# Two weight splits moved from GpSimd to ScalarE and VectorE: gate's first unit, and v and k of the second attention

## What is computed

```python
h = rms_norm(x, pre_norm_gain);  q, k, v, z_a, b, c, u, z_c = split(h @ w_in)
attn = rms_norm(diff_attention(q, k, v)) * silu(z_a);  conv_out = b * conv(c * u) * silu(z_c)
mixed = concat(attn, conv_out) @ w_out
x = x + rms_norm(mixed, post_norm_gain)                 # x1
e = rms_norm(p @ w_ple_proj, ple_norm_gain)
x = x + sigmoid(x @ w_ple_gate) * e                     # x2
```

```python
y = gmlp(rms_norm(x, a_pre_g)) @ a_w_out                # a
h = x + rms_norm(y, a_post_g)                           # h3
kv = rms_norm(h, kv_norm_g);  k, v = kv @ w_k, kv @ w_v # k5, v5: 256 columns each
q, z = split(rms_norm(h, b_pre_g) @ b_w_in)             # q5, z5
out = h + rms_norm((swa(q, k, v) * silu(z)) @ b_w_out, b_post_g)
```

## Time and profile before

| | us |
|---|---|
| median of 3 runs | 880.46 |
| lowest, highest | 880.06, 880.82 |
| the profiled execution | 880.86 |
| its span, first to last instruction | 879.1 |
| TensorE busy | 863.0 (98%) |
| VectorE busy | 574.7 (65%) |
| GpSimd busy | 510.2 (58%) |
| ScalarE busy | 385.3 (44%) |

### The profile page before, as it was taken

One profiled execution on the slowest core, in us unless ns is written; L12 is line 12 of the kernel. 1 busy time (PEld: TensorE's weight loads), 2 busy tenths in 40 slices (PEclk: granted clock), 3 DMA queues, 4 the chain that ended last, 5 costly groups with the idle time before them and its releaser, 6 DMA issues.

```text
span 879.1 us, 11945 instructions
## 1 busy us (share of the span) xinstructions
PE 863.0 (98%) x4196; PEld 718.9 (82%) x4196; DVE 574.7 (65%) x918; ACT 385.3 (44%) x830; POOL 510.2 (58%) x564
## 2 busy tenths in 40 slices
PE   8999999999999999999999999999997999999997
PEld 6888888888887788888888888888887888888885
DVE  6125648875998389676766625556995467788624
ACT  4123333433665377555112311113775446667622
POOL 7766555682248822319974048772369797566352
PEclk9999999999999999999999999999999999999999
DMA  7543222453952468994742254526961222112202
GB/s 199 167 121 97 72 79 66 142 121 72 236 197 71 144 144 181 218 231 150 170 121 86 88 168 108 133 80 163 213 181 60 72 80 89 49 48 73 72 1 95
DMA packets 83691, 106.84 MB, mean 122 GB/s; under 512 B 11953, under 2 KB 54449, under 8 KB 83634
## 3 DMA queue, kind: packets, MB, share of 16 engines
q1 hardware_dynamic: 72752, 85.12, 30.5%
q0 software_dynamic: 10880, 20.97, 14.1%
q10 hardware_dynamic: 2, 0.00, 0.0%
HBM read 103.98 MB, written 2.10 MB: 121 GB/s over the span
## 4 chain that ended last, share of the span: by engine, by line
PE 88%; POOL 4%; DVE 4%; issue 1%; ACT 1%; DMA 1%; POOLq 0%; DVEq 0%; ACTq 0%
PE bank L2192 26%; PE bank L2194 26%; PE bank L2193 26%; PE bank L2436 2%; PE bank L2464 1%; DMA raw<-in_w_out 1%; DVE acc L1747 1%; PE bank L2289 1%; POOL wlo L873 1%; PE bank L2409 1%; PE bank L2459 1%; PE bank L2458 1%; DVE resid L1751 1%; POOL ms L818 1%; POOL whi L864 1%
## 5 line engine op out<-in xcount | busy, mean ns | idle before, releaser
L873 POOL TENSOR_TENSOR wlo<-raw,whi 128x512 fp32r<-128x512 f32 x184 | 254.8, 1417 | 3.9 <-ACT whi L1052 3.2
L864 POOL TENSOR_SCALAR whi<-raw 128x512 fp32r<-128x512 f32 x174 | 122.8, 746 | 175.7 <-PE bank L2194 170.1
L2192 PE MATMUL bank<-actB_hi,whi 128*128 128x512 f32 (+1 forms) x416 | 159.6, 384 | 0.6 <-POOL wlo L873 0.6
L2193 PE MATMUL bank<-actB_lo,whi 128*128 128x512 f32 (+1 forms) x416 | 158.6, 381 | 0.0
L2194 PE MATMUL bank<-actB_hi,wlo 128*128 128x512 f32 (+1 forms) x416 | 158.5, 381 | 0.0
L2192 PE MATMUL bank<-whi,actA_hi 128*128 128x512 f32 x350 | 138.0, 394 | 1.0 <-DVE actA_lo L1496 1.0
L2194 PE MATMUL bank<-whi,actA_lo 128*128 128x512 f32 x350 | 136.4, 390 | 0.0
L2193 PE MATMUL bank<-wlo,actA_hi 128*128 128x512 f32 x350 | 136.2, 389 | 0.0
L2192 PEld LDWEIGHTS bank<-actB_hi,whi 128*128 128x128 f32 x416 | 78.3, 188 | 15.5 <-issue 1.4
L2194 PEld LDWEIGHTS bank<-actB_hi,wlo 128*128 128x128 f32 x416 | 78.2, 188 | 15.2
L2193 PEld LDWEIGHTS bank<-actB_lo,whi 128*128 128x128 f32 x416 | 78.3, 188 | 14.2
(11 more groups left out here) (273 smaller groups left out, 1636.3 us busy)
## 6 DMA issues: line engine op xcount, KB each, us to landing
raw<-in_a_w_in SPq DMA_DIRECT2D x44, 512.0 KB, 4.3
raw<-in_w_in SPq DMA_DIRECT2D x32, 512.0 KB, 3.9
raw<-in_b_w_in SPq DMA_DIRECT2D x16, 512.0 KB, 3.4
raw<-in_a_w_out SPq DMA_DIRECT2D x12, 512.0 KB, 3.5
gain<-in_a_w_out POOLq DMA_DIRECT2D x9, 512.0 KB, 8.6
raw<-in_w_ple_gate SPq DMA_DIRECT2D x8, 512.0 KB, 4.6
gain<-in_a_w_in POOLq DMA_DIRECT2D x8, 512.0 KB, 7.0
raw<-in_a_w_in POOLq DMA_DIRECT2D x8, 512.0 KB, 7.4
```

What stands on the lines that cost most here:

```text
L864: pool.tensor_scalar(H, src[:, i * HALF:(i + 1) * HALF], 1.0, 1.0, ALU.mult, ALU.mult).then_inc(w_hi, 1)
L873: ins = pool.tensor_tensor(L, src[:, i * HALF:(i + 1) * HALF], H.bitcast(f32), ALU.subtract)
L2192: M(out_, whi_, xhi_, start=start, stop=False)
L2193: M(out_, whi_, xlo_, start=False, stop=False)
```

## The change

Two units change their path, and orders around them change with it.

- gate 0 goes to the path of ScalarE and VectorE (`hi_two`, and two `lo_two` ahead of `post`). GpSimd's roots of m1 (the sum that x1 needs) and its mask of w_s now all stand before gate 1.
- v5 and k5 go to that path as well. v5 is loaded into a room of its own, V (`smC` and `gcv`), right after a10's load. ScalarE scales v5 between the copies for a8, a9 and a10, copies it after a10, and scales k5 around the copy for a12. VectorE subtracts v5 after the residual of tile 1 and k5 after the low parts of n0 and a later gain. GpSimd runs its eight roots in a row.
- v5's loads wait for a11's to land and k5's for v5's, since they share the counts `room_in`, and GpSimd's scaling waits for a count of `w_scaled`.
- Orders: the block n0 of TensorE moves between the two blocks of a13, n1 stays behind it. On VectorE, sums, gains and residuals of each tile move closer together, and a13's second subtraction behind the first residual. On ScalarE, the copies of a13's two halves come behind the squares that the first roots need.

```diff
@@ weight tables
 BY_TWO = [n for n, u in enumerate(UNITS) if u[2] == "S"
-          or u[:2] in (("ple", 0), ("z4", 0), ("z4", 4))]
-TWO_NO = {n: k for k, n in enumerate(BY_TWO)}
+          or u[:2] in (("ple", 0), ("gate", 0), ("z4", 0), ("z4", 4))]
+V5_K5 = [n for s in ("v5", "k5") for n, u in enumerate(UNITS) if u[0] == s]
+HI_NO = {n: k for k, n in enumerate(BY_TWO[:-3] + V5_K5[:1] + BY_TWO[-3:] + V5_K5[1:])}
+TWO_NO = {n: k for k, n in enumerate(BY_TWO + V5_K5)}
@@ tensor_order
-        o += [("A", n, r) for n in (range(4), range(4, 14))[half] for r in range(2)]
-    o += turn("n", 0) + turn("n", 1) + [("v5", 0), ("v5", 1)]
+        o += [("A", n, r) for n in (range(4), range(4, 13))[half] for r in range(2)]
+    o += [("A", 13, 0)] + turn("n", 0) + [("A", 13, 1)] + turn("n", 1) + [("v5", 0), ("v5", 1)]
@@ room_place
+                    "V": gcv[:, :, :].rearrange("p a b -> p (a b)")[:, 0:D] if h else smC[:, :],
@@ SyncE, load_half
+                elif s == "v5":
+                    sp.wait_ge(s4_bias, KA)
+                    sp.wait_ge(zu_made, KA)
+                    sp.wait_ge(raw_in[10 + h], LANDED[UNIT_NO["a", 11], h])
...
+                if s == "k5":
+                    sp.wait_ge(raw_in[10 + h], LANDED[UNIT_NO["v5", 0], h])
@@ GpSimd, order
-            after[at("gate", 0, 1)] = [lambda: root("m1", 2, D), lambda: root("m1", 3, D), mask_ws]
...
-            after[at("zc", 1, 1)] += [lambda: root("m1", 0, D), lambda: root("m1", 1, D)]
+            after[at("zc", 1, 1)] += [lambda t=t: root("m1", t, D) for t in range(T)] + [mask_ws]
...
-            after[at("v5", 0, 1) - 0.25] = [lambda: root("a", 0, D), lambda: root("a", 1, D)]
...
+            after[at("u4", 7, 1)] += [lambda n=n, t=t: root(n, t, D) for n, t in (
+                ("a", 0), ("a", 1), ("h3", 0), ("h3", 1), ("a", 2), ("a", 3), ("h3", 2), ("h3", 3))]
@@ ScalarE
-            hi_gate(UNIT_NO["gate", 0])
+            hi_two(UNIT_NO["gate", 0])
...
+            def hi_v5():
+                act.wait_ge(pe_block, BLOCK["s4", KA - 1])
+                act.wait_ge(s4_bias, KA)
+                act.wait_ge(w_scaled, 8)
+                for h in range(2):
+                    A(v5hi[:, h * D:(h + 1) * D], raw_of(UNIT_NO["v5", 0], h)[0], ACT.Copy).then_inc(w7_hi, 1)
+
+            def hi_k5(h):
+                n = UNIT_NO["k5", 0]
+                act.wait_ge(pe_block, last_block(SLOT_BEFORE[n]))
+                act.wait_ge(w_scaled, 8 + 4 * (h + 1))
+                A(halves_of(n, 2 * h, 2)[0], raw_of(n, h)[0], ACT.Copy).then_inc(w7_hi, 1)
@@ VectorE, gate and the end of a
+            for h in range(2):
+                lo_two(UNIT_NO["gate", 0], h)
             dve.wait_ge(gain_in[1], 16)
...
+            add_kept(5, 0, a_out_(0, 1), a_out_(0, 1), (c7_made, 42 + 7))
             part_gain(3, 1)
...
+            add_kept(5, 1, a_out_(1, 1), a_out_(1, 1), (c7_made, 42 + 11))
+            part_gain(0, 1)
             lo_a(13, (0,))
-            part_gain(0, 1)
+            h3_in(0)
+            part_gain(1, 1)
             lo_a(13, (1,))
...
+            for h in range(2):
+                lo_two(UNIT_NO["v5", 0], h)
```

More of the change, by code:

```diff
@@ L110, in room_of @@
         return "K"
-    k = WHOLE[n] if n < UNIT_NO["v5", 0] else WHOLE[n] + (s == "v5")
+    if s == "v5":
+        return "V"
+    k = WHOLE[n]
     return "AB"[k % 2]
@@ L857, in split_half @@
                     pool.wait_ge(pe_block, last_block(SLOT_BEFORE[u]))
-                if s == "v5":
-                    pool.wait_ge(pe_block, BLOCK["s4", KA - 1])
-                    pool.wait_ge(s4_bias, KA)
-                    pool.wait_ge(zu_made, KA)
-                for i in range(2 if n and (s, UNITS[u][1]) not in (("gate", 0), ("gate", 1)) else 0):
+                for i in range(2 if n and (s, UNITS[u][1]) != ("gate", 1) else 0):
                     H, _ = halves_of(u, 2 * (n % 2) + i)
@@ L941, in _ @@
             after[at("u4", 7, 1)] = [lambda n=n: add_a(n) for n in (7, 8, 9, 12, 13)]
-            after[at("v5", 0, 1) - 0.25] = [lambda: root("a", 0, D), lambda: root("a", 1, D)]
-            after[at("v5", 0, 1)] = [lambda: root("h3", 0, D)]
-            after[at("k5", 0, 0) - 0.5] = [lambda: root("h3", 1, D)]
-            after[at("k5", 0, 1) - 0.5] = [lambda: root("a", 2, D)]
-            after[at("k5", 0, 1)] = [lambda: root("a", 3, D), lambda: root("h3", 2, D)]
-            after[at("q5", 0, 0) - 0.5] = [lambda: root("h3", 3, D)]
+            after[at("u4", 7, 1)] += [lambda n=n, t=t: root(n, t, D) for n, t in (
+                ("a", 0), ("a", 1), ("h3", 0), ("h3", 1), ("a", 2), ("a", 3), ("h3", 2), ("h3", 3))]
             for n in range(2 * len(UNITS)):
@@ L1221, in copied_h, with hi_a @@
                       ACT.Copy).then_inc(h_copied, 1)
-            def hi_a(n):
+            def hi_v5():
[9 more added lines that the diff above has]
+                A(halves_of(n, 2 * h, 2)[0], raw_of(n, h)[0], ACT.Copy).then_inc(w7_hi, 1)
+            def hi_a(n, halves=(0, 1)):
                 u = UNIT_NO["a", n]
                 act.wait_ge(pe_block, last_block(SLOT_BEFORE[u]))
-                for h in range(2):
+                for h in halves:
                     act.wait_ge(*ready_a(n, h))
@@ L1397, in _ @@
             rows_hi(actA_hi, 0, "22", hi["y4"])
+            scale_two("v5", 0)
             hi_a(9)
@@ L1400, in _ @@
             square_a(1, 0)
+            scale_two("v5", 1)
             hi_a(10)
+            hi_v5()
             hi_a(11)
             square_a(2, 1)
-            scale_two("v5", 0)
+            scale_two("k5", 0)
             hi_a(12)
             square_a(3, 1)
-            scale_two("v5", 1)
-            scale_two("k5", 0)
-            hi_a(13)
+            scale_two("k5", 1)
             square_a(0, 1)
+            hi_a(13, (0,))
             square_a(1, 1)
-            scale_two("k5", 1)
+            hi_a(13, (1,))
             h3_out(0)
+            hi_k5(0)
+            normed_n(0)
             h3_out(1)
-            normed_n(0)
+            turned_n(0)
             normed_n(1)
-            turned_n(0)
             square_a(2, 0)
+            hi_k5(1)
             turned_n(1)
@@ L2049, in _ @@
             lo_a(12)
+            add_kept(5, 0, a_out_(0, 1), a_out_(0, 1), (c7_made, 42 + 7))
             part_gain(3, 1)
-            for r in range(2):
-                add_kept(5, r, a_out_(r, 1), a_out_(r, 1), (c7_made, 42 + 4 * r + 7))
+            add_kept(5, 1, a_out_(1, 1), a_out_(1, 1), (c7_made, 42 + 11))
+            part_gain(0, 1)
             lo_a(13, (0,))
-            part_gain(0, 1)
+            h3_in(0)
+            part_gain(1, 1)
             lo_a(13, (1,))
-            part_gain(1, 1)
-            h3_in(0)
             h3_in(1)
+            for h in range(2):
+                lo_two(UNIT_NO["v5", 0], h)
             add_kept(6, 0, p03_kept(0), a_out_(2, 0), (c7_made, 42 + 6))
+            rest_n(0)
+            lo_two(UNIT_NO["k5", 0], 0)
             add_kept(6, 1, p03_kept(1), a_out_(3, 0), (c7_made, 42 + 10))
-            rest_n(0)
             part_gain(2, 0)
+            h3_in(2)
             rest_n(1)
-            h3_in(2)
             part_gain(3, 0)
+            lo_two(UNIT_NO["k5", 0], 1)
             h3_in(3)
```

23 lines of the change are left out of this document (11 added, 12 removed).

## The result

The changed kernel takes 882.24 us (median of 19 runs, 880.25 to 884.55) against 880.52 of the kernel before (19 runs, 880.06 to 881.66). The ratio is 1.0018, with a 95% interval of 1.0011 to 1.0024. So it is slower by 1.7 us, a small loss whose interval lies clear of no change, where I had forecast 3.6 us less. The profiled execution took 881.42 us, its span is 879.7, 0.6 longer than that of before. It is one of the quicker ones of the changed kernel (0.8 under its median), and the profiled one of before lay 0.3 above its own, so the medians differ by 1.2 us more than the two traces do.

The account below looks back on a forecast made before the run. TensorE, busy 863.0 of 879.1 us, bounds the kernel, so only its idle time can be won: 880.86 minus 1.75 (front) minus 1.8 (tail) is 877.3; the median lies 0.4 lower, so 876.9 us, range 874.6 to 879.8.

Parts of the forecast that it names:

- The front edit: Before the transposes of x1's fourth tile: TensorE's wait goes whole, minus 1.75 us, bounds 1.2 and 1.95.
- a gap before 650: Sign of being wrong: TensorE gets an idle gap before 650 us on the timeline.
- k5's scaling ahead of a12: ScalarE's copy for a12 stands behind k5's scaling and load; a12's first half still in time by 0.4 us.
- The sign named for it: Copy for a12 on ScalarE starting later than 649, on the clock before, means rivals 2 or 4 hold.
- Rival 2: v5's early load collides with a9's load and delays a12: 1.0 to 1.4 us back, 878.1; chance 0.18.
- Rival 4: k5's late load holds up a12 through ScalarE's scaling: 5.7 us late gives 882.2 or more; chance 0.05.
- A root at 1.8 us: GpSimd's root of the first tile, before n0, takes 1.8 us; TensorE's wait there is 0.9 instead of 1.71.
- Rival 3: Roots starve behind VectorE's subtractions: 1.2 us more at each of three roots, 880.5, no change; chance 0.10.
- (a): a13's second half, subtracted behind the first residual and a gain: a new TensorE wait of 0.6 to 1.2 us.
- (c): Before n1: ready at about 665.5 against 664.7, a TensorE wait of 0.75 us.
- (d): v5's first block loses its 0.70 us wait; the second gets a new wait of 1.0.
- The gaps before n2, n3 and v5's third block: n2 and n3 are ready before TensorE comes, so waits of 1.14, 0.24 and the second 0.70 us go.

Follow-up runs that it names:

- gate_alone: The kernel before with only the front edit (gate 0 on ScalarE and VectorE), the end of a untouched: 879.09 us against 880.72, ratio 0.9984.
- v5_light: The changed kernel with v5's early load cut to a quarter, so its output is not valid: 880.25 us against 880.43, ratio 0.9995.
- after_wait: The changed kernel with one added wait: VectorE starts v5's subtractions only after the root of h3 of tile 0: 877.82 us, ratio 0.9968.
- k5_behind: The changed kernel with k5's first half scaled behind the copy for a12 and the squares of tile 3: 875.81 us, ratio 0.9949.

## Why the prediction was wrong, step by step

- **The front edit, -1.75: the wait went whole, but the net gain at TensorE is 1.3.** gate_alone measured -1.6, within the bounds of 1.2 and 1.95, part of it by luck (above). x1 of tile 0 was ready at 260.2 (predicted 260.45; the whole trace is 0.2 earlier there), each of the four instructions that were line 1751 (1769 now) took 1.22 or 1.23. The free pair of line 1747 took 1.41, where I had 1.28. What I had missed is the 0.39 at 293, where TensorE waits for GpSimd's subtraction; why it is late there I did not follow up. It is also a gap before 650, which I had named as a sign of being wrong.

```profile
255.29 2.35 DVE L1689 TENSOR_TENSOR wlo<-raw,whi 128x1024 fp32r<-128x1024 f32 x2
257.56 1.41 DVE L1765 SCALAR_TENSOR_TENSOR acc<-big,rstd,gain 128x512 f32<-128x512 f32 x2
259.00 1.22 DVE L1769 TENSOR_TENSOR resid<-resid,acc 128x1024 f32<-128x1024 f32 x1
...
269.51 1.23 DVE L1769 TENSOR_TENSOR resid<-resid,acc 128x1024 f32<-128x1024 f32 x1
```

- **k5's scaling ahead of a12, "in time by 0.4": failed.** The step of the prediction that failed is the issue of k5's load. I took 642.54 less the front's shift, though I had written myself that a delay of a9 would pass through VectorE to a11's room, and priced that at 0 for the sum. It came 1.9 us late, and v5_light gives all of it back. Less the 0.4 of slack this is 1.5, the gap of 1.54. The sign named for it came: the copy for a12 starts at 648.75, on the clock of before 650.1, later than 649.
- **Rival 2, the load that collides: its mechanism was right, its end wrong.** I let it cost 1.0 to 1.4; alone it costs 2.0 here (v5_light), but only because ScalarE's list waits for k5's load ahead of a12's copy. The rule of the Trainium skill ("DMA: Bandwidth & Descriptors", "Queues, rings and completion order"), that a DMA engine takes turns between the queues that have work, is what the runs agree with: a9's load, on another queue, took 9.8 us beside v5's 1 MB and 7.4 beside a quarter of it. That v5's packets stand behind a10's and that a9's load is on another queue were my reasons for 0; neither kept a9's load clear of v5's.
- **Rival 4, slower through k5's scaling: right in mechanism, mis-sized.** I wanted the load 5.7 us late for a slower kernel, since I let the rest of the tail gain as forecast. It was 1.9 late, which is 1.5 of the loss.
- **A root at 1.8 us: failed, and it is the largest term (0.9 forecast for the gap before n0, 3.62 measured).** The root of h3 of tile 0 took 4.74. Rival 3 had this, at 1.2 us a root and 880.5. I held against it that v5's pair stands "between two of them". It stood right behind the residual of tile 1, and the root of tile 0 was not yet through then: by my own times it started at 658.1 and the residual of tile 1 ended near 660. The loss was one root with two subtractions of 1.2 each, not 1.2 at each of three. The Trainium skill ("SBUF — State Buffer", "Who interferes with whom") says that a VectorE instruction with two SBUF inputs and a GpSimd one that reads SBUF exclude each other for the whole of an instruction. The traces agree and show more than that: "rstd" took until the end of three VectorE instructions in a row (the second of the residual and v5's two), not of one.
- **The clock behind n0: not in the prediction.** 1.3 us in the profiled run, since I forecast no gap above 1.2.
- **(a), the wait in a13: right**, 0.65 for 0.6 to 1.2. **(c)** n1: none, as n0 was so late. **(d)** 0.43 for 1.0. **The gaps before n2, n3 and v5's third block: gone, as said. The gap in q5: 0.59, as said.**

With v5's subtractions off the root, after_wait is 3.0 us under the kernel before, where the sum said 3.55; k5_behind is at 4.9. In k5_behind's trace the gaps of the tail sum to 1.93, a gain of 3.4 where I had 1.8. The gains were there; k5's scaling ahead of a12's copy, together with v5's early load, and v5's subtractions beside the root took them back.
